# A PEER expert stage cut in two phases: U partly as dense products, V alone afterwards

## What is computed

```
q = (h @ w_q).reshape(tokens, 8, 2, 128)
s1, s2 = q[..., 0, :] . k1, q[..., 1, :] . k2          # 128 scores each
v1, i1 = top_k(s1, 16); v2, i2 = top_k(s2, 16)
score, pos = top_k(v1[:, None] + v2[None, :], 16)      # of 256 candidates
idx = (i1 * 128 + i2)[pos]; gate = softmax(score)
act = gelu(w_u[idx] . h)                               # w_u: 16384 x 2048
out = sum over heads and k of (gate * act) * w_v[idx]  # w_v: 16384 x 2048
```

## Time and profile before

| | us |
|---|---|
| median of 3 executions | 3165.56 (3165.32 to 3170.72) |
| the profiled execution, its own time | 3173.48 |
| its span, first to last instruction | 3171.7 |
| PE busy | 2708.2 (85%) |
| VectorE busy | 1949.5 (61%) |
| ScalarE busy | 936.7 (30%) |
| GpSimd busy | 598.8 (19%) |

### The profile page before, as it was taken

One profiled execution on the slowest core, in us unless ns is written; L12 is line 12 of the kernel. 1 busy time (PEld: TensorE's weight loads), 2 busy tenths in 40 slices (PEclk: granted clock), 3 DMA queues, 4 the chain that ended last, 5 costly groups with the idle time before them and its releaser, 6 DMA issues.

```text
span 3171.7 us, 33622 instructions
## 1 busy us (share of the span) xinstructions
PE 2708.2 (85%) x11665; PEld 1856.2 (59%) x11665; DVE 1949.5 (61%) x2602; ACT 936.7 (30%) x1257; POOL 598.8 (19%) x580
## 2 busy tenths in 40 slices
PE   8899997998887999999999636968778778788778
PEld 3488775878675889999878513434334334343323
DVE  2389996433766777888555566555556565655652
ACT  1167775431454443333443200101111111111100
POOL 0000000000000000000000153534343434443341
PEclk9999998999999999999999868999989899999999
DMA  8633334542211877888556499999999999999996
GB/s 325 225 122 117 108 117 146 192 152 80 94 68 64 345 307 290 342 318 319 199 200 244 178 388 412 416 421 409 422 409 422 399 422 409 421 399 422 421 421 272
DMA packets 126334, 906.72 MB, mean 286 GB/s; under 512 B 13984, under 2 KB 15264, under 8 KB 16416
## 3 DMA queue, kind: packets, MB, share of 16 engines
...
HBM read 901.33 MB, written 4.23 MB: 286 GB/s over the span
## 4 chain that ended last, share of the span: by engine, by line
PE 48%; DMA 28%; DVE 10%; issue 9%; ACT 3%; POOL 1%; DVEq 0%; ACTq 0%; POOLq 0%
DMA u<-in_peer_u,idx 27%; PE ps L424 12%; PE ps L467 6%; PE ps L468 6%; PE ps L469 6%; PE ps L760 6%; PE ps L482 3%; PE ps L439 2%; DVE u L1619 2%; PE ps L642 1%; DVE wl L1134 1%; PE ps L624 1%; DVE ub L1218 1%; POOL v L1692 1%; DVE tt L1229 1%
## 5 line engine op out<-in xcount | busy, mean ns | idle before, releaser
L760 PE MATMUL ps<-v,dg 128*128 128x512 f32 x2048 | 929.2, 610 | 199.1 <-DMA v<-in_peer_v,idx 100.0
L1619 DVE SCALAR_TENSOR_TENSOR u<-u,hN 128x2048 f32<-128x2048 f32 x256 | 586.5, 2292 | 486.8 <-DMA u<-in_peer_u,idx 474.9
L760 PEld LDWEIGHTS ps<-v,dg 128*128 128x128 f32 x2048 | 391.3, 195 | 732.7 <-issue 571.6
L1134 DVE TENSOR_TENSOR wl<-w,wh 128x1024 fp32r<-128x1024 f32 x432 | 525.1, 1222 | 373.9 <-ACT wh L805 373.1
L805 ACT ACTIVATE wh<-w 128x1024 fp32r<-128x1024 f32 x432 | 453.2, 1058 | 731.9 <-PE ps L469 317.7
L424 PE MATMUL ps<-both,wh 128*128 128x256 f32 x2560 | 475.6, 288 | 5.4 <-DVE y L1343 5.1
L1685 POOL DMA_INDIRECT u<-in_peer_u,idx x256 | 281.8, 1101 | 886.7 <-DVE u L1619 459.6
L424 PEld LDWEIGHTS ps<-both,wh 128*128 128x128 f32 x2560 | 404.6, 194 | 17.1 <-issue 15.0
L424 PE MATMUL ps<-both,wl 128*128 128x256 f32 x1280 | 363.5, 284 | 0.0
L1090 ACT ACTIVATE dg<-con,wt 128x128 f32<-128x128 f32 x256 | 99.1, 399 | 852.2 <-PE ps L760 846.9
L1692 POOL DMA_INDIRECT v<-in_peer_v,idx x256 | 282.7, 1104 | 188.4 <-PE ps L760 104.8
...
...
## 6 DMA issues: line engine op xcount, KB each, us to landing
...
u<-in_peer_u,idx POOLq DMA_INDIRECT x256
v<-in_peer_v,idx POOLq DMA_INDIRECT x256, 18.0
...
```

The costliest lines, as they stand in the source:

```text
L760: last = mm(ps[:, b, :], dg[:, k % 4, :], V[n % NV][:, b * 512:(b + 1) * 512], start=(k == 0), stop=(k == TOPK - 1))
L1134: tt(wl[p % SPLITS][:, :, :], W[s][:, q * PIECE:(q + 1) * PIECE, :], wh[p % SPLITS][:, :, :].bitcast(F32), ALU.subtract)\
L1619: stt(U[n % NU][:, :], U[n % NU][:, :], 1.0, hN[:, t, :], ALU.mult, ALU.mult, accum_out=dot[:, t, k:k + 1])\
```

## The change

The expert stage is cut in two phases.

**Phase 1.** The first 1,024 of U's 2,048 columns are no longer gathered. They are laid out on the host as 32 chunks of 512 experts (2 MiB each), join the stream after and between the query weights, and PE multiplies *all* 16,384 experts with `hT` (`all_experts`: 16 matmuls of 128x512 a chunk). ScalarE copies each chunk's products from PSUM to a staging tile and stores it in DRAM (`a_rows`, 2 x 128 x 16,384). `PLAN` is the order of queries ("q"), scores ("s") and chunks ("u") on PE and ScalarE. The other 1,024 columns are gathered (0.5 MiB a gather, 8 buffers `U`) and dotted on VectorE beside the routing of a head ahead. All gathers of U come first on GpSimd; seven rows of V are fetched behind them. Routing results (`idx`, the unnormalized `gate`, `dot`) stay in SBUF for all heads. Keys come in one load. `x2` stays in SBUF, its DRAM round trip and the clearing of `acc` go.

**Phase 2.** When all products are stored and all dots done, GpSimd gathers the chosen 4-byte products back from DRAM (`spot_of`: 256 indirect DMAs of 128 x 4 bytes into `dense`), in turn with the V rows (16 buffers `V`). VectorE adds the two halves of each dot, makes weights, and takes 7 of each 16 V rows itself (`row`: multiply by the weight and add to `acc`); PE takes the other 9, and keeps its sums in all 8 PSUM banks until the end, so that `add` disappears. The host code gives U in two parts; loops are unrolled.

The diff, cut to its core:

```diff
+DK = 8
+DD = DK * P
+UCH = EXPERTS // WIDE
+HALVES = WQ0 + 2 * PH + 2 * UCH
...
+PLAN, _c = [("q", 0), ("s", 0), ("q", 1), ("s", 1), ("u", 0), ("q", 2), ("u", 1), ("s", 2)], 2
+for _h in range(3, PH):
+    PLAN += [("u", _c), ("u", _c + 1), ("q", _h), ("u", _c + 2), ("s", _h), ("u", _c + 3)]
+    _c += 4
+PLAN += [("u", _n) for _n in range(_c, UCH)]
+LOADS = [x for x in PLAN if x[0] != "s"]
...
-        x2_dram = nc.dram_tensor("x2_rows", [2, P, D], F32, kind="Internal").ap()
+        a_dram = nc.dram_tensor("a_rows", [2, P, EXPERTS], F32, kind="Internal").ap()
+        a_flat = a_dram.rearrange("t p (e o) -> (t p e) o", o=1)
...
-        NU, NV = 4, 8
-        U = [sb(f"u{i}", R_HX + 16384 + 8192 * i, [P, D]) for i in range(NU)]
+        NU, NV, NS = 8, 16, 3
+        U = [sb(f"u{i}", at, [P, D - DD]) for i, at in enumerate(
+            [R_HX + 16384 + 4096 * i for i in range(4)] + [R_BR + 16384 + 4096 * i for i in range(4)])]
         V = [sb(f"v{i}", at, [P, D]) for i, at in enumerate(
-            [R_SPLIT + 8192 * i for i in range(4)] + [R_HX, R_HX + 8192, R_Y + 8192, R_Y + 16384])]
-        acc = sb("acc", R_HX + 16384 + 8192 * NU, [P, 2, D])
+            [R_SPLIT + 8192 * i for i in range(4)] + [R_BR, R_BR + 8192, R_Y + 8192] + [8192 * i for i in range(4)]
+            + [R_HC, R_HC + 8192, R_HX + 16384, R_HX + 24576, R_BR + 16384])]
+        V_EARLY, V_KEYS = 7, 4
+        stage = [sb(f"stage{i}", at, [P, 2, WIDE]) for i, at in enumerate((R_Y, R_Y + 4096, R_E))]
+        acc = sb("acc", R_HC + 16384, [P, 2, D])
...
+        ON_DVE = (1, 3, 5, 7, 9, 11, 13)
+        ON_PE = tuple(k for k in range(TOPK) if k not in ON_DVE)
+
+        def row_used(r):
+            n, k = divmod(r, TOPK)
+            return (dve_rows, n * len(ON_DVE) + ON_DVE.index(k) + 1) if k in ON_DVE else (pe_rows, n * len(ON_PE) + ON_PE.index(k) + 1)
...
+                if h >= 2:
+                    pe.wait_ge(*VR.at(h - 2, "ib1_1"))
+                pe.wait_ge(keys_in, 16)
...
+            def all_experts(c, n):
+
+                if c >= 2:
+                    pe.wait_ge(dense_copied, c - 1)
+                for q, w in halves_of(n):
+                    wv = w[:, :, :].rearrange("p (k a) n -> p k (a n)", a=2)
+                    for kk in range(4):
+                        k = q * 4 + kk
+                        for t in (0, 1):
+                            last = mm(ps[:, 2 * (c % 2) + t, :], hT[:, k, t * P:(t + 1) * P], wv[:, kk, :], start=(k == 0), stop=(k == DK - 1))
+                    last.then_inc(piece_used, 2)
+
+            pe.wait_ge(*VW.at(NW // 2 - 1, "m11"))
+            for what, i in PLAN:
+                if what == "s":
+                    scores(i)
+                elif what == "q":
+                    queries(i, LOADS.index((what, i)))
+                else:
+                    all_experts(i, LOADS.index((what, i)))
...
+            pe.wait_ge(dense_copied, UCH)
+            pe.wait_ge(*VR.at(PH - 1, "ib1_1"))
+            for n in range(2 * PH):
+                t = n % 2
+                for j, k in enumerate(ON_PE):
+                    r, i = n * TOPK + k, n * len(ON_PE) + j
+                    pe.wait_ge(v_in[r % NV], 16 * (r // NV + 1))
+                    pe.wait_ge(diagonals_done, i + 1)
+                    for b in range(4):
+                        last = mm(ps[:, 4 * t + b, :], dg[:, i % 4, :], V[r % NV][:, b * WIDE:(b + 1) * WIDE],
+                                  start=(n == t and j == 0), stop=(n >= 2 * PH - 2 and j == len(ON_PE) - 1))
+                        if n == 2 * PH - 1 and j == len(ON_PE) - 1 and b < 3:
+                            last.then_inc(last_bank, 1)
+                    last.then_inc(pe_rows, 1)
...
-                act.dma_start(x2_dram[t], x2[:, t, :]).then_inc(x2_stored, 16)
...
+            act.wait_ge(*VF.at(0, "g1"))
+            act.dma_start(keys[:, :, :, :], a_keys.rearrange("h p (s n) -> p h s n", s=2)).then_inc(keys_in, 16)
...
+            for what, i in PLAN:
+                if what == "s":
+                    continue
+                act.wait_ge(piece_used, 2 * WQ0 + 4 * (LOADS.index((what, i)) + 1))
+                if what == "q":
+                    if i:
+                        act.wait_ge(*PR.at(i - 1, "s1"))
+                    fn(qT[:, :, :], ps[:, 4, :].rearrange("p (s t) -> p s t", s=2), ACT.Copy).then_inc(*AR.inc("q"))
+                    if i >= 3:
+                        gates(i - 3)
+                else:
+                    if i >= NS:
+                        act.wait_ge(staged_out[i % NS], 16 * (i // NS))
+                    fn(stage[i % NS][:, :, :], ps[:, 2 * (i % 2):2 * (i % 2) + 2, :], ACT.Copy).then_inc(dense_copied, 1)
+                    act.wait_ge(dense_copied, i + 1)
+                    act.dma_start(a_dram[:, :, i * WIDE:(i + 1) * WIDE].rearrange("t p e -> p t e"), stage[i % NS][:, :, :])\
+                        .then_inc(staged_out[i % NS], 16)
+                    if i == UCH - 3:
+                        gates(PH - 3)
...
+            gates(PH - 2)
+            gates(PH - 1)
...
+            gelu(0)
+            for n in range(2 * PH):
+                act.wait_ge(weights_done, n + 1)
+                for j, k in enumerate(ON_PE):
+                    i = n * len(ON_PE) + j
+                    if i >= 4:
+                        act.wait_ge(pe_rows, i - 3)
+                    fn(dg[:, i % 4, :], ident, ACT.Copy, scale=wt[:, n % 2, k:k + 1]).then_inc(diagonals_done, 1)
+                    if j == 2 and n + 1 < 2 * PH:
+                        gelu(n + 1)
...
-                dve.wait_ge(*PR.at(h, f"s{t}"))
+                dve.wait_ge(*PR.at(h, "s1"))
...
+            def dots(n, routed=(), many=1):
+
+                h, t = divmod(n, 2)
...
+                    dve.wait_ge(u_in[r % NU], 16 * (r // NU + 1))
+                    stt(U[r % NU][:, :], U[r % NU][:, :], 1.0, hN[:, t, DD:D], ALU.mult, ALU.mult, accum_out=dot[:, t, h, k:k + 1])\
+                        .then_inc(dots_done, 1)
...
+            for _ in route(0, 0):
+                pass
+            dots(0, itertools.chain(route(0, 1), route(1, 0)), 2)
+            for n in range(1, 2 * PH):
+                dots(n, route(*divmod(n + 2, 2)) if 2 < n + 2 < 2 * PH else ())
+                if n == 2 * PH - 3:
+                    for t in (0, 1):
+                        dve.wait_ge(*VR.at(PH - 1, f"ef_{t}"))
+                        tsc(spot[:, t, :, :], tef[:, t, :, :], base[:, t:t + 1], None, ALU.add).then_inc(spots_done, 1)
...
+            def activations(n):
+
+                h, t = divmod(n, 2)
+                dve.wait_ge(dense_in[n % 4], 16 * TOPK * (n // 4 + 1))
+                dve.wait_ge(dots_done, (n + 1) * TOPK)
...
+                tt(d, dot[:, t, h, :], dense[:, t, h, :], ALU.add).then_inc(*VE.inc("g0"))
...
+            def row(n, j):
+
+                r, t = n * TOPK + ON_DVE[j], n % 2
+                i = n * len(ON_DVE) + j
+                dve.wait_ge(v_in[r % NV], 16 * (r // NV + 1))
+                dve.wait_ge(weights_done, n + 1)
...
+                    stt(acc[:, t, :], V[r % NV][:, :], w, acc[:, t, :], ALU.mult, ALU.add).then_inc(dve_rows, 1)
...
+            activations(0)
+            weights(0)
+            for n in range(2 * PH):
+                for j in range(len(ON_DVE)):
+                    row(n, j)
+                    if n + 1 < 2 * PH:
+                        if j == 1:
+                            activations(n + 1)
+                        if j == 3:
+                            weights(n + 1)
+                    elif j == 2:
+                        final0()
...
+            def row_u(r):
...
+                if r >= NU:
+                    pool.wait_ge(dots_done, r - NU + 1)
                 apart(pool)
-                nc.gpsimd.indirect_dma_start(out=U[n % NU][:, :], out_offset=None, in_=a_u,
-                                             in_offset=bass.IndirectOffsetOnAxis(ap=idx[:, odd, t, k:k + 1], axis=0)).then_inc(u_in[n % NU], 16)
-
-            def rows_v(h, odd, t, k):
-                n = t * TOPK + k
-                pool.wait_ge(*(PE_.at(h, "v%d%d" % divmod(n - NV, TOPK)) if n >= NV else PE_.at(h - 1, f"v1{TOPK - NV + k}")))
+                nc.gpsimd.indirect_dma_start(out=U[r % NU][:, :], out_offset=None, in_=a_u,
+                                             in_offset=bass.IndirectOffsetOnAxis(ap=idx[:, t, h, k:k + 1], axis=0)).then_inc(u_in[r % NU], 16)
...
+            def spot_of(r):
+
+                n, k = divmod(r, TOPK)
+                h, t = divmod(n, 2)
+                if n >= 4 and k == 0:
+                    pool.wait_ge(weights_done, n - 3)
+                apart(pool)
+                nc.gpsimd.indirect_dma_start(out=dense[:, t, h, k:k + 1], out_offset=None, in_=a_flat,
+                                             in_offset=bass.IndirectOffsetOnAxis(ap=spot[:, t, h, k:k + 1], axis=0)).then_inc(dense_in[n % 4], 16)
+
+            pool.wait_ge(*VF.at(0, "ha11"))
```

(42 more changed lines are left out.)

314 lines of the change are left out of this document (136 added, 178 removed).

## The result

The changed kernel takes **3,183.9 us** (median of 5 runs, 3,182.8 to 3,185.4) against 3,166.7 us for the kernel before beside it (3,165.3 to 3,173.0): a ratio of **1.0048, interval 1.0036 to 1.0060**, so half a per cent slower. The forecast was 3,187 us.

The account below looks back on a forecast made before the run. DMA transfers bound the old expert stage; now DMA bounds phase 1 (to 2,396 us), GpSimd issues phase 2. Adding 53 us, 14 blocks (679 us) and the end gives 3,195 us; against the median 3,187 us, range 3,105 to 3,290 us.

Parts of the forecast that it names:

- Phase 1's end: U phase, bound by the DMA: 571 us of packets from 1,806.4 us plus losses, ending at 2,396 us, 25 us either way.
- the loss on top: Phase 1's DMA: 8 us lost in the first 100 us of gathers, 1.5% more for holes while VectorE routes.
- PE beside it: PE in phase 1: dense products 455 us, queries 112 us, scores 16 us, ending near 2,362 us, inside the DMA's time.
- rival C: Phase 1 runs 40 us over, by PE at clock 0.89 or 4 KB packets at 177 ns: about 3,227 us; chance 0.13.
- The block: Phase 2, 16 V rows: 32 GpSimd issues take 40.0 us, VectorE's rows holding gathers add 8.5 us: 48.5 us.
- The tail: Phase 2's end: 6 us until block 15's activations, 53 us of PE rows, 1.5 us last bank, 4.3 us store.
- Rival A: Phase 2: gathers rarely meet VectorE rows, so the DMA sets blocks of 44.5 us: 3,131 us; chance 0.30.
- point of decision: Phase 2: from a block of 47.0 us down, 1.5 us under the forecast's, the change turns from slower to faster.
- Rival B: Phase 2: random 4-byte reads are dear, at 110 ns a block takes 54.4 us: 3,270 us; chance 0.15.
- The estimate by the Trainium skill: Phase 2's scalar gathers priced by packet count: 1.34 us each, 21.5 us a block, about 3,373 us; chance 0.05.
- The signs to look for: Five trace signs, among them first scalar gather about 2,397 us, phase 2 DMA share below 0.95, block period 48.5 us.

Follow-up runs that it names:

- e6: Changed kernel without the scalar gathers and without phase 1's 32 stores of dense products to DRAM: 2,987.7 us, ratio 0.9426 to the kernel before.
- e4: Changed kernel without the 256 scalar gathers and the wait for them, the dot added to itself instead: 3,025.9 us, ratio 0.9546 to the kernel before.
- e8: e2 with eight of 16 V rows on VectorE in the last two blocks: 3,163.6 us, ratio 0.9988 to the kernel before.
- e3: Changed kernel with VectorE's rows taking one input from PSUM instead of SBUF, sums wrong: 3,137.3 us, ratio 0.9903 to the kernel before.
- e7: Changed kernel with phase 2 doing tile 0 then tile 1, VectorE adding its rows in PSUM, everything computed: 3,139.3 us, ratio 0.9908 to the kernel before.
- e10: Changed kernel with the edits of e7 and e9 together, nothing else: 3,070.4 us, ratio 0.9682 to the kernel before.
- e1: Changed kernel with VectorE taking 4 of each 16 V rows instead of 7, PE 12: 3,186.3 us, ratio 1.0054 to the kernel before.
- e2: Changed kernel with VectorE taking 5 of each 16 V rows instead of 7, PE 11: 3,186.9 us, ratio 1.0048 to the kernel before.
- e9: Changed kernel with the next block's scalars issued two at a time behind the first eight V rows: 3,187.0 us, ratio 1.0046 to the kernel before.
- e11: e10 with eight instead of seven VectorE rows in the last two blocks: 3,069.3 us, ratio 0.9677 to the kernel before.
- e5: Changed kernel gathering only the scalars of odd k, 8 a block, each used twice: 3,084.1 us, ratio 0.9734 to the kernel before.

## Why the prediction came out

The direction and the cause held. That the size did too is in good part luck. Phase 1 ended 23 us early, the blocks ran 9 us and the tail 2 us late: the sum was 11.5 us too long. Of this the 7.9 us took most away that the forecast subtracts because the profiled execution of before lay above its median; the one of after lies 0.4 us under its own. With the right end of phase 1 and all else as forecast, the sum would have given 3,164 us, no change at all. The two profiled executions differ by 10.0 us, the medians by 17.2 us, where 21.5 us were forecast.

- **Phase 1's end, 23 us early.** The first scalar gather was to start at about 2,397 us and started at 2,374.0 us. The prices held: from 1,900 to 2,300 us the 4 KB packets took 163 ns by the queue's share (I took 162), the 2 KB packets of the stores 84 ns (85), and all stores together 41.5 us by e6 against e4 (44). The failed step was the loss on top, 8 us for the first 100 us and 1.5% for holes while VectorE routes. The two dips of the earlier trace rows did not come back, perhaps since they belonged to the old start with its late second scores. In after the share is 0.95 in the first 100 us and then 1.02, so there were no holes to speak of, and the 571 us of packets, counted at a share of 1.00, passed in 567 us (1,806.0 to 2,372.9). Here the lesson is that a share of 1.00 is not the ceiling of this counter.
- **PE beside it.** The products ended at 2,337.5 us (2,362 forecast), with the granted clock at 1.00 all the way. So the start of rival C, a clock of 0.89 with PE this full, didn't occur, and its other start, 4 KB packets at 177 ns, didn't either. That PE and the DMA are close was right: in e6 PE is the one that ends last.
- **The block, 49.2 us for 48.5.** 32 issues of 1.25 us are 39.9 us. Of the long gathers there are 103, about seven a block as forecast, and each costs 2.27 - 0.94 = 1.33 us, where I had booked 8.5 / 7 = 1.21 us. 39.9 + 7 x 1.33 = 49.2 us. The mis-sized term is mainly the first long gather of a burst: over the 15 bursts it takes 2.66 us on average (2.03 to 3.04 us, by how soon behind the start of the row it starts), the others 2.2 us. Over 14 blocks all of this is 9 us.
- **The tail, 66.8 us for 65.** From 3,114.7 to 3,181.5 us. PE runs 15 rows without a wait behind the last activations, as forecast; they took 53.6 us for 15 x 3.55 = 53.3:

```profile
3121.54 53.55 PE L822 MATMUL ps<-v,dg 128*128 128x512 f32 x120 [14.44 <-ACT dg L1161]
```

- **Rival A** (gathers and rows rarely meet) had 0.30 and fell: today's gathers wait for the dots, the new ones don't wait, and so nearly every row of VectorE catches one. Its point of decision, 47.0 us a block, was taken with the late end of phase 1; from the measured times it is 49.2 - 17.2/14 = 47.9 us. e8, with a block of 47.9 us, has a ratio of 0.9988, and at 45.8 and 46.1 us (e3, e7) there is a gain of 1%.
- **Rival B** (dear scalar reads) fell as well. A block's rows and scalars pass at 408 to 409 GB/s in e10 and at 421 GB/s without scalars in e4, 3% of 40 us or 1.2 us a block; I had 3.8 us. Nearly all of it is that the packets of 8 KB take longer, 322 ns on average in e10 against 314 ns in e4. The queue's packet counts speak of this too: from 2,450 to 3,000 us after has 8,640 packets under 512 B, e4 3,528. Of e4's there are 16 for each V row (231 MB, 220 rows). Taking 16 as well for each of after's 180 rows and 180 scalar gathers leaves 2,880, which is 16 for a scalar gather of 128 values, one an engine. These are records of 32 bytes, eight scalars, and take 13 ns each. My 128 packets an engine and block are 16 in the records. The estimate by the Trainium skill (DMA: Bandwidth & Descriptors, "Measured"), 10.5 ns for each packet taken one behind the other, had given 21.5 us a block. The trace doesn't agree with that use of it.
- **The signs to look for** all came: first scalar gather behind the last dot, DMA share below 0.95 (0.90), GpSimd idle for nothing but its 0.3 us, gathers at a mean near 1.2 us, VectorE in bursts, the last 15 rows without a wait.

For the mechanism behind the block: the Trainium skill (SBUF — State Buffer, "Who interferes with whom") says that a VectorE instruction with at most one SBUF input, outside its 2-port modes, doesn't contend with GpSimd, and one with two does with a GpSimd instruction that reads SBUF. e3, e7 and e10 agree, with 1 to 2 long gathers of 464 where after has 103.

**Open.** Why PE's signals come late in e1, e2, e3, e7 and e8, and in step with the rows in e4, e9, e10 and e11, no run says. The traces of after and e5 miss 28 and 18 of the 144 signals, so there it can't be told; GpSimd hardly waits for them. PE's granted clock of 0.50 delays its first rows in e3 by some 3 us, but GpSimd's waits begin behind the end of those rows. Nor does any run say whether a held gather waits in reading its list of indices or elsewhere; only the durations are measured.
